# A subtraction on GpSimd in four pieces of 256 columns instead of one of 1024

## The chip and the metric

The kernel runs on one core of a Trainium2 chip. Its time is the device time of one execution in microseconds. In the profile PE is TensorE (PEld its weight loads), DVE is VectorE, ACT is ScalarE, POOL is GpSimd, and SP is SyncE, which only issues DMAs here.

## What is computed

One layer of a hybrid decoder over 512 tokens of width 1024, in float32:

```
h = rms_norm(x, norm_mix)
(hq, hf, hi, hg, nq, kc, vc, ksl, vsl, kwn, vwn, ngate, gate_a, gate_b) = split(h @ w_in)
y_a = hgrn2_mixer(hq, hf, hi, hg, ...) @ w_branch_a
y_b = nsa_mixer(nq, kc, vc, ksl, vsl, kwn, vwn, ngate, ...) @ w_branch_b
mixed = sigmoid(gate_a) * y_a + sigmoid(gate_b) * y_b
x = x + mixed @ w_out
h = rms_norm(x, norm_mlp)
x = x + square(relu(h @ w_up)) @ w_down
```

`hgrn2_mixer` is a gated linear recurrence with 4 heads of 128; `nsa_mixer` is causal attention with 8 query heads, 2 key/value heads of 64 and three branches (compressed blocks, selected blocks, window). `w_in` has 6936 columns, `w_up` is 1024 x 4096, `w_down` 4096 x 1024.

## The kernel before

All weights pass through the core as 127 **chunks** of 128 partitions x 1024 columns of float32 (512 KB), in a fixed order. A matmul in float32 is made of three in the faster type `fp32r`: an operand is split into a high part (rounded to `fp32r`) and a low part (what is left), and `three()` (L362 to L366) multiplies high x high, high x low and low x high into one PSUM bank. A chunk of a plain projection (`project()`, L368) holds eight tiles of 128 x 128 and gives 24 matmuls of 512 columns.

A chunk goes through three engines:
- SyncE loads it into one of four slots of `wraw` (L274), once the chunk four before has been split (`w_split`).
- GpSimd splits it (`split()`, L291): a copy to `whi` in `fp32r` (L292), a wait for that copy (`w_hi`), and a subtraction `wlo = wraw - whi` (L294), whose end raises `w_split`. `whi` and `wlo` have two slots each, so a split begins only when TensorE has used the chunk two before (`w_used`, L300 and L342), and runs while TensorE works on the chunk in between. Chunk 1 has code of its own, in halves of 512 columns (L305 to L311). In the attention stage GpSimd's queue also holds 64 `scale` steps (L327) between some of the splits.
- TensorE waits for `w_split` (`take()`, L352; in the loops of the MLP L773 and L805).

The order of the chunks: `f0 q0 f1 q1 f2 q2 f3 q3`, `i0` to `i3`, `kc vc ks kw nq0` to `nq3`, `m0` to `m2`, `g0 c00 g1 c01 g2 c10 g3 c11`, `ga0` to `ga7`, `gb0` to `gb7`, `ab0` to `ab7`, `wo0` to `wo7`, and 64 of the MLP in two halves of 16 up and 16 down. "Chunk 2" is `f1`. A `c` chunk gives only eight short matmuls (`hidden()`, L575), `m2` only 24 of 280 columns.

VectorE's work around this, as far as it is spoken of below:
- The first sums of squares, L1100 and L1101; a fold of a constant, L1113.
- `start_head()` (L1126 to L1132): the gates of the recurrence for one head. `scaled()` (L1108) reads a finished projection out of PSUM and frees its bank; the next projection but one waits for that (`claim()`, L355).
- `advance()` (L1172): one level of the recurrence, three multiplications in SBUF: L1180 (totals), L1182 (`k_dec`, 1024 elements) and L1183 (`q_dec`, 1024 elements). Behind it stand `keep_near` (L1190), `norm` (L1214) and `leave_stat` (L1221), which frees the bank that a later statistics matmul (L388) of TensorE claims.
- In `ab` and `wo`: L1451 adds the two gated branches, ACT rounds the sum to `hhi` (L1041), `mix_low` (L1439) forms the low part; the first `wo` chunk waits for `mix_lo` before each of its eight tiles.
- In the up stages: L1485 (from PSUM), L1487 (two inputs in SBUF), then ACT's rounding (L1063) and L1490 (two inputs in SBUF).

Of the kernel before, what the change touches and what calls it, by code (L numbers as in the profile page):

```python
# [25 lines left out]
F32 = mybir.dt.float32  # L26
# [3 lines left out]
ALU = mybir.AluOpType  # L30
# [47 lines left out]
def build_block(nc, xT, w, oh, masks, ident_in, small_in, w2, rel, scratch, skewed, out):  # L78
    with ExitStack() as ctx:
        base = (nc.sbuf_base + 31) // 32 * 32  # L80

        def at(name, kb, shape, dt=F32):

            return nc.alloc_sbuf_tensor_at(name, shape, dt, offset=base + int(kb * 1024))

        def sem(name):
            return ctx.enter_context(nc.semaphore(name))
# [16 lines left out]
        wraw = at("wraw", 36.5, [P, NRAW, CW])  # L104
        wsp = at("wsp", 52.5, [P, 2, NSPLIT, CW], F32R)
        whi, wlo = wsp[:, 0], wsp[:, 1]
# [75 lines left out]
        w_split = sem("w_split")  # L182
# [82 lines left out]
        def p_tile(t, g, n):  # L265
            return p_ring[:, t % 4, g, 0:n] if t % 4 < 3 else p_last[g][:, 0:n]
# [4 lines left out]
        @block.sync  # L271
        def _(sp):
            def load(c, slot):
                sp.dma_start(wraw[:, slot, :], w[c]).then_inc(w_landed[slot], 16)  # L274

            load(0, 0)
            for n in range(4):
                sp.dma_start(x0[:, 2 * n:2 * n + 2, :], xT[:, 2 * n:2 * n + 2, :]).then_inc(x_in[n], 16)
            for c in range(1, FIRST):
                if c >= NRAW:  # L280
                    sp.wait_ge(w_split, c - NRAW + 1)
                load(c, c % NRAW)
            with sp.Fori(0, (N_CHUNKS - FIRST) // 4) as i:
                for j in range(4):
                    sp.wait_ge(w_split, 4 * i + (FIRST + j - NRAW + 1))
                    load(4 * i + (FIRST + j), (FIRST + j) % NRAW)


        @block.gpsimd
        def _(pool):  # L290
            def split(c, raw, two):  # L291
                pool.tensor_scalar(whi[:, two, :], wraw[:, raw, :], 1.0, 0.0, ALU.mult, ALU.add).then_inc(w_hi, 1)  # L292
                pool.wait_ge(w_hi, c + 1)
                pool.tensor_tensor(wlo[:, two, :], wraw[:, raw, :], whi[:, two, :].bitcast(F32),  # L294
                                   ALU.subtract).then_inc(w_split, 1)

            def split_straight(c):
                pool.wait_ge(w_landed[c % NRAW], 16 * (c // NRAW + 1))
                if c >= NSPLIT:
                    pool.wait_ge(w_used, c - NSPLIT + 1)  # L300
                split(c, c % NRAW, c % NSPLIT)

            split_straight(0)
            pool.wait_ge(w_landed[1], 16)
            for half in range(2):  # L305
                c = slice(512 * half, 512 * half + 512)
                pool.tensor_scalar(whi[:, 1, c], wraw[:, 1, c], 1.0, 0.0, ALU.mult, ALU.add).then_inc(
                    half_split, 1)
                pool.wait_ge(half_split, 2 * half + 1)
                pool.tensor_tensor(wlo[:, 1, c], wraw[:, 1, c], whi[:, 1, c].bitcast(F32), ALU.subtract).then_inc(  # L310
                    half_split, 1)  # L311
            pool.wait_ge(half_split, 4)
            pool.sem_inc(w_hi, 1)
            pool.sem_inc(w_split, 1)
            for c in range(2, AT["gb2"] + 1):
                split_straight(c)


            def scale(t):
                gi, qb = divmod(t, 4)  # L320
                i, b = divmod(gi, 2)
                n = (qb + 1) * P
                pool.wait_ge(w_ready, t + 1)
                for g in range(2):
                    p_ = p_tile(t, g, n)
                    c = 3 * (4 * g + i) + 1 + b
                    pool.tensor_scalar(p_, p_, rinv[:, t % 4, g:g + 1], gate3[:, qb, c:c + 1], ALU.mult, ALU.mult  # L327
                                       ).then_inc(p_scaled[g], 1)

            for t in range(NT + 2):  # L330
                if t in GB_AFTER:
                    split_straight(AT[GB_AFTER[t]] + 1)
                if t < NT:
                    scale(t)
            for c in range(AT["gb7"] + 2, POOL_FIRST):
                split_straight(c)

            with pool.Fori(0, (N_CHUNKS - POOL_FIRST) // 4) as i:
                for j in range(4):
                    c = POOL_FIRST + j  # L340
                    pool.wait_ge(w_landed[c % NRAW], 16 * i + 16 * (c // NRAW + 1))
                    pool.wait_ge(w_used, 4 * i + (c - NSPLIT + 1))  # L342
                    pool.sem_inc(w_open, 1)
                    split(4 * i + c, c % NRAW, c % NSPLIT)
# [1272 lines left out]
```

## Time and profile before

| | |
|---|---|
| median of 3 runs | 817.58 us (817.57 to 817.68) |
| the profiled execution | 817.72 us, of which the span from first to last instruction is 815.9 us |
| PE busy | 799.5 us, 98% of the span |
| PEld busy | 635.4 us, 78% |
| POOL busy | 490.3 us, 60% |
| DVE busy | 414.9 us, 51% |
| ACT busy | 193.9 us, 24% |
| granted TensorE clock | 1.000 throughout |

A timeline row gives the start and the duration of an instruction in microseconds, the engine, its line, what it writes and reads with shapes, how many were merged into the row, and in brackets how long the engine was idle before it and what released it. A duration of an instruction includes time in which it was issued but held up. Matmuls overlap, so PE's pace is read from the starts of rows that follow each other: 0.23 us for 512 columns.

### The profile page before, as it was taken

To read this page: it belongs to the slowest core of one execution; us is meant where nothing else is said; L and a number is where in the kernel's file an instruction comes from. 1 tells how busy PE (TensorE), PEld (TensorE's weight loads), DVE (VectorE), ACT (ScalarE), POOL (GpSimd) and SP (SyncE) were. 2 spreads that over 40 slices of the span, in tenths; PEclk is the share of its full clock that TensorE was granted. 3 is DMA by queue.
4 is the path that set the end of the run, shared out by engine and by line. 5 is a ranking of instruction groups with operands and counts; after the bars stand their busy time and mean duration, and the time that the engine had idled before them with its cause. 6 is when DMAs were issued, how large, how long until landed. Compare 5 with 4: busy or idle time off the path is not lost.

```text
span 815.9 us, 12340 instructions
## 1 busy us (share of the span) xinstructions
PE 799.5 (98%) x4632; PEld 635.4 (78%) x4632; DVE 414.9 (51%) x565; ACT 193.9 (24%) x397; POOL 490.3 (60%) x324
## 2 busy tenths in 40 slices
PE   8999999998999999999999999999999999999998
PEld 6788877987778566567878888888888888888886
DVE  6696485834465454543887766672000376650000
ACT  5100753312411455545112122220000122210000
POOL 4656644567454565464666666666666666776663
PEclk9999999999999999999999999999999999999999
DMA  7334221233422100004223222223332233233320
GB/s 248 105 126 168 96 79 55 78 116 117 154 78 78 53 27 27 27 27 181 98 84 103 99 83 103 90 90 104 103 100 82 101 104 98 82 103 129 119 86 26
DMA packets 22973, 78.01 MB, mean 96 GB/s; under 512 B 2659, under 2 KB 2923, under 8 KB 22804
## 3 DMA queue, kind: packets, MB, share of 16 engines
q1 hardware_dynamic: 18864, 68.69, 24.8%
q10 hardware_dynamic: 4068, 8.75, 3.0%
q8 instruction: 29, 0.48, 0.2%
q14 instruction: 12, 0.10, 0.0%
HBM read 75.31 MB, written 4.21 MB: 97 GB/s over the span
## 4 chain that ended last, share of the span: by engine, by line
PE 90%; DVE 5%; POOL 2%; DMA 1%; issue 1%; ACT 1%; SPq 0%; DVEq 0%; POOLq 0%; ACTq 0%
PE bank L364 25%; PE bank L366 24%; PE bank L365 24%; PE bank L694 3%; PE bank L706 3%; PE bank L727 2%; PE bank L444 1%; PE bank L446 1%; PE bank L445 1%; DMA wraw<-in_w 1%; PE bank L388 1%; POOL wsp L294 1%; DVE f L1129 1%; PE bank L493 1%; PE bank L716 1%
## 5 line engine op out<-in xcount | busy, mean ns | idle before, releaser
L294 POOL TENSOR_TENSOR wsp<-wraw,wsp 128x1024 fp32r<-128x1024 f32 x126 | 309.6, 2457 | 10.5
L292 POOL TENSOR_SCALAR wsp<-wraw 128x1024 fp32r<-128x1024 f32 x126 | 136.6, 1084 | 255.7 <-PE bank L366 165.3
L364 PE MATMUL bank<-hhi,wsp 128*128 128x512 f32 x352 | 141.2, 401 | 7.3 <-POOL wsp L294 2.5
L365 PE MATMUL bank<-hlo,wsp 128*128 128x512 f32 x352 | 137.4, 390 | 0.0
L366 PE MATMUL bank<-hhi,wsp 128*128 128x512 f32 x352 | 137.3, 390 | 0.0
L364 PE MATMUL bank<-ghi,wsp 128*128 128x512 f32 x256 | 100.3, 392 | 0.0
L366 PE MATMUL bank<-ghi,wsp 128*128 128x512 f32 x256 | 99.7, 390 | 0.0
L364 PE MATMUL bank<-uhi,wsp 128*128 128x512 f32 x256 | 99.7, 389 | 0.0
L365 PE MATMUL bank<-glo,wsp 128*128 128x512 f32 x256 | 99.7, 389 | 0.0
L365 PE MATMUL bank<-ulo,wsp 128*128 128x512 f32 x256 | 99.6, 389 | 0.0
L366 PE MATMUL bank<-uhi,wsp 128*128 128x512 f32 x256 | 99.6, 389 | 0.0
L364 PEld LDWEIGHTS bank<-hhi,wsp 128*128 128x128 f32 x352 | 66.0, 188 | 28.0 <-issue 6.4
L366 PEld LDWEIGHTS bank<-hhi,wsp 128*128 128x128 f32 x352 | 66.1, 188 | 14.3
L365 PEld LDWEIGHTS bank<-hlo,wsp 128*128 128x128 f32 x352 | 66.2, 188 | 12.5
L1487 DVE TENSOR_TENSOR u_ring<-t_ring,r_ring 128x512 f32<-128x512 f32 x32 | 57.2, 1787 | 1.1
L364 PEld LDWEIGHTS bank<-ghi,wsp 128*128 128x128 f32 x256 | 48.0, 188 | 11.9 <-issue 1.5
L364 PEld LDWEIGHTS bank<-uhi,wsp 128*128 128x128 f32 x256 | 48.1, 188 | 10.2 <-issue 0.3
L366 PEld LDWEIGHTS bank<-ghi,wsp 128*128 128x128 f32 x256 | 48.1, 188 | 10.1
L366 PEld LDWEIGHTS bank<-uhi,wsp 128*128 128x128 f32 x256 | 48.1, 188 | 10.1
L365 PEld LDWEIGHTS bank<-ulo,wsp 128*128 128x128 f32 x256 | 48.1, 188 | 9.9
L365 PEld LDWEIGHTS bank<-glo,wsp 128*128 128x128 f32 x256 | 48.1, 188 | 9.7 <-issue 0.2
L1490 DVE TENSOR_TENSOR ulo<-u_ring,uhi 128x512 f32 x32 | 38.6, 1206 | 32.5 <-ACT uhi L1063 32.5
(241 smaller groups left out, 1024.5 us busy)
## 6 DMA issues: line engine op xcount, KB each, us to landing
wraw<-in_w SPq DMA_DIRECT2D x127, 512.0 KB, 3.2
x<-in_xT SPq DMA_DIRECT2D x4, 512.0 KB, 7.5
bias_skewed<-bias_lines ACTq DMA_DIRECT2D x1, 2048.0 KB
bias<-bias_skewed ACTq DMA_DIRECT2D x1, 2048.0 KB, 9.0
x<-in_xT ACTq DMA_DIRECT2D x1, 2048.0 KB, 8.4
out<-x ACTq DMA_DIRECT2D x8, 256.0 KB, 2.0
cst<-in_w ACTq DMA_DIRECT2D x1, 96.0 KB
ohs<-in_oh ACTq DMA_DIRECT2D x1, 82.5 KB
```

Source lines behind the costliest of these rows:

```text
L292: pool.tensor_scalar(whi[:, two, :], wraw[:, raw, :], 1.0, 0.0, ALU.mult, ALU.add).then_inc(w_hi, 1)
L294: pool.tensor_tensor(wlo[:, two, :], wraw[:, raw, :], whi[:, two, :].bitcast(F32), ALU.subtract).then_inc(w_split, 1)
L364: pe.matmul(out_, wh, mh, start=first, stop=False)
L365: pe.matmul(out_, wh, ml, start=False, stop=False)
L366: return pe.matmul(out_, wl, mh, start=False, stop=last)
L388: pe.matmul(to[:, 0:n], matrix, squares, start=True, stop=True).then_inc(stat_out, 1)
L444: pe.matmul(to, hh, wh[:, c], start=k == 0, stop=False)
L694: pe.matmul(score_bank(t, g)[:, 0:n], qn[rows, i, qb * P:qb * P + P], keys[b][rows, 0:n], start=True, stop=True).then_inc(s_done[g], 1)
L706: last = pe.transpose(bank[4 + g][:, kb * P:kb * P + P], p_tile(t, g, S)[:, kb * P:kb * P + P], ident[:])
L727: last = pe.matmul(bank[6][64 * g:64 * g + 64, 256 * half + c:256 * half + 256], v_sw[:, kb, b * P + g * 64:b * P + g * 64 + 64], pt[:, g, ...
L1487: dve.tensor_tensor(u_ring[:, s, :], t_ring[:, s, :], r_ring[:, s, :], ALU.mult).then_inc(u_f, 1)
L1490: dve.tensor_tensor(ulo[:, 4 * i + j, :], u_ring[:, s, :], uhi[:, 4 * i + j, :].bitcast(F32), ALU.subtract).then_inc(u_lo, 1)
```

## The change

The subtraction of `split()` is issued as four instructions of 256 columns each, one behind the other without a wait between them, and the last of them raises `w_split`. The bytes read and written, the semaphores and their counts are the same. `split()` serves 126 of the 127 chunks; chunk 1, which has its own code, is as before. The copy of L292 stays one instruction of 1024 columns. The lines behind it move down by two: the subtraction is L296 in the changed kernel.

```diff
                 pool.wait_ge(w_hi, c + 1)
-                pool.tensor_tensor(wlo[:, two, :], wraw[:, raw, :], whi[:, two, :].bitcast(F32),
-                                   ALU.subtract).then_inc(w_split, 1)
+                for n in range(4):
+                    q = slice(256 * n, 256 * n + 256)
+                    last = pool.tensor_tensor(wlo[:, two, q], wraw[:, raw, q], whi[:, two, q].bitcast(F32), ALU.subtract)
+                last.then_inc(w_split, 1)
```

## Rows read from the trace of the kernel before

**Rows 1.** The page, busy time, share of the span and instructions of each engine.

```profile
PE 799.5 (98%) x4632; PEld 635.4 (78%) x4632; DVE 414.9 (51%) x565; ACT 193.9 (24%) x397; POOL 490.3 (60%) x324
```

**Rows 2.** Pool's groups by form: busy us, mean ns, idle before.

```profile
L294 POOL TENSOR_TENSOR wsp<-wraw,wsp 128x1024 fp32r<-128x1024 f32 x126 | 309.6, 2457 | 10.5
...
L327 POOL TENSOR_SCALAR p_ring<-p_ring,cst 128x128 f32<-128x128 f32 x16 | 7.0, 447 | 4.8 <-DVE cst L1401 4.5
```

**Rows 3.** Timeline of POOL, first subtraction of chunk 1 and the copy behind it.

```profile
14.52 1.28 POOL L310 TENSOR_TENSOR wsp<-wraw,wsp 128x512 fp32r<-128x512 f32 x1
...
15.76 1.61 POOL L307 TENSOR_SCALAR wsp<-wraw 128x512 fp32r<-128x512 f32 x1
```

**Rows 4.** Timeline of DVE in the same stretch.

```profile
15.05 3.38 DVE L1100 TENSOR_TENSOR xsq<-xsq 128x1024 f32<-128x1024 f32 x2 [1.10 <-ACT xsq L854]
...
16.92 3.73 DVE L1100 TENSOR_TENSOR xsq<-xsq 128x1024 f32<-128x1024 f32 x2
```

**Rows 5.** Timelines of PE (chunks started as their split ends) and POOL.

```profile
24.36 0.50 PE L364 MATMUL bank<-hhi,wsp 128*128 128x512 f32 x1 [0.56 <-POOL wsp L294]
...
168.45 0.58 PE L364 MATMUL bank<-hhi,wsp 128*128 128x512 f32 x1
...
177.98 0.50 PE L364 MATMUL bank<-hhi,wsp 128*128 128x512 f32 x1
...
187.45 0.50 PE L364 MATMUL bank<-hhi,wsp 128*128 128x512 f32 x1 [0.37 <-POOL wsp L294]
...
196.88 0.50 PE L364 MATMUL bank<-hhi,wsp 128*128 128x512 f32 x1 [1.54 <-POOL wsp L294]
...
165.68 2.35 POOL L294 TENSOR_TENSOR wsp<-wraw,wsp 128x1024 fp32r<-128x1024 f32 x1
...
175.58 2.35 POOL L294 TENSOR_TENSOR wsp<-wraw,wsp 128x1024 fp32r<-128x1024 f32 x1
```

**Rows 6.** Timelines of POOL, DVE and PE where g0 is split.

```profile
155.70 2.40 POOL L294 TENSOR_TENSOR wsp<-wraw,wsp 128x1024 fp32r<-128x1024 f32 x1
...
155.87 2.25 DVE L1180 TENSOR_TENSOR tot<-tot 128x8 f32<-128x8 f32 x1 [1.16 <-PE bank L530]
...
158.04 1.21 DVE L1182 TENSOR_TENSOR k_dec<-k_dec,tot 128x1024 f32<-128x1024 f32 x1
...
159.17 2.06 DVE L1183 TENSOR_TENSOR q_dec<-q_dec,tot 128x1024 f32<-128x1024 f32 x1
...
158.75 0.40 PE L364 MATMUL bank<-hhi,wsp 128*128 128x512 f32 x1
```

**Rows 7.** Timelines of DVE and PE, two statistics matmuls.

```profile
108.75 2.05 DVE L1180 TENSOR_TENSOR tot<-tot 128x512 f32<-128x512 f32 x1 [0.63 <-PE bank L493]
...
114.86 0.67 PE L388 MATMUL bank<-sq,pair_ones 128*128 128x512 f32 x1 [0.57 <-DVEq L1221]
...
139.28 1.10 PE L388 MATMUL bank<-sq,pair_ones 128*128 128x512 f32 x2
```

**Rows 8.** Timelines of DVE and PE, the wait at 53.96.

```profile
50.48 1.95 DVE L1130 SCALAR_TENSOR_TENSOR k_dec<-e,f 128x512 f32<-128x512 f32 x1
...
53.96 0.47 PE L364 MATMUL bank<-hhi,wsp 128*128 128x512 f32 x1 [0.33 <-DVEq L1111]
```

**Rows 9.** Timelines of DVE and PE, the wait in wo0.

```profile
419.55 2.87 DVE L1451 TENSOR_TENSOR rstd<-gates 128x512 f32<-128x512 f32 x1
...
423.07 0.50 PE L364 MATMUL bank<-hhi,wsp 128*128 128x512 f32 x1 [0.86 <-DVE hlo L1439]
```

**Rows 10.** Timelines of PE and POOL in an up stage.

```profile
485.42 0.39 PE L364 MATMUL bank<-ghi,wsp 128*128 128x512 f32 x1
...
490.86 0.43 PE L364 MATMUL bank<-ghi,wsp 128*128 128x512 f32 x1
...
485.78 1.06 POOL L292 TENSOR_SCALAR wsp<-wraw 128x1024 fp32r<-128x1024 f32 x1 [1.30 <-PE bank L366]
...
492.56 2.81 POOL L294 TENSOR_TENSOR wsp<-wraw,wsp 128x1024 fp32r<-128x1024 f32 x1
```

## The prediction

> **What bounds the kernel now.** I read four views. First the page: TensorE is busy for 98% of the span, so nearly every microsecond is matmul time that this change doesn't touch; it can only widen or narrow the roughly 16 us in which PE stands idle [rows 1]. Second, Pool's group: the subtraction that is cut is one row of 126 instructions of 2.46 us on average, 309.6 us in all [rows 2]. A chunk feeds 24 matmuls, which take 5.44 us (PE starts chunks at 485.42 and 490.86), and one copy and one subtraction fit in that; so most splits have slack, and an average says nothing. Third, the timeline of PE: which chunks does it start the moment their subtraction ends? Fourth, the timelines of DVE and Pool side by side, since the two hold each other up.
>
> **What the rows show of Pool against DVE.** The first `L1100` on DVE (both inputs in SBUF) is issued at 15.05, while Pool's 512-column subtraction runs from 14.52 to 15.80; the next `L1100` starts at 16.92, so the first took 1.9 us [rows 3, 4]. The work alone is about 1.1 us (1024 columns take 1.21 with what surrounds them [rows 6]), thus it ran from 15.80 to 16.92, held until Pool's instruction ended. Pool's next instruction, `L307`, has no wait ahead of it and was issued at 15.76, yet took 1.61 us, against 1.06 for a copy of twice its width elsewhere [rows 10]: it was held by DVE in turn.  So: a DVE instruction with two SBUF inputs and a Pool instruction exclude each other whole, and DVE gets in at the boundary between two Pool instructions even when these stand back to back. DVE instructions that read PSUM are not held. That is the mechanism of this change. It makes four boundaries of one: DVE's waits get shorter, and Pool's split, with up to three DVE instructions let in, gets longer.
>
> The Trainium skill, "SBUF — State Buffer", section "Who interferes with whom", says the same of the lock: one DVE instruction with two SBUF inputs and a GpSimd one that reads SBUF fully block each other for a whole instruction. It adds that issue order decides; that is rival B below.
>
> **Cost of the cut itself.** Undisturbed, 512 columns take 1.28 us and 1024 take 2.35 [rows 3, 5], so 2.09 ns a column and 0.21 us fixed; with 2.40, as elsewhere [rows 6], 0.16 fixed. A 256-column piece is then 0.73 to 0.75 us. Back-to-back Pool instructions overlap by 0.04 (15.76 against 15.80) [rows 3]. Four pieces: 2.80 to 2.88 us, 0.4 to 0.53 over the uncut one. I take +0.5 us a chunk. Ends: 0 if the start of a piece hides wholly under the one before, and +0.95 if each has the 0.32 us that `L327` leaves (447 ns for 128 columns, less 128 at the copy's 1.0 ns) [rows 2]. Of about 63 us more on Pool nearly all lies under matmuls. On the path it stands at these places:
> - Chunk 2 (PE at 24.36, 0.56 idle on `L294`), `g3` (187.45, 0.37 idle) and `ga0` (196.88, 1.54 idle) are waited for; `g2` at 177.98 starts 0.05 after its subtraction ends (175.58 + 2.35 = 177.93) [rows 5]. Each pays 0.5, chunk 2 and `ga0` 0.05 more for small DVE instructions let in (`L1113` and `L1114`; `L1300`): 2.1.
> - `g1` starts at 168.45 and its subtraction ends at 168.03 (165.68 + 2.35): 0.42 of slack, less 0.06 of signal; 0.5 costs 0.15.
>
> The Trainium skill, "GPSIMD Engine Reference", section "2.1 Instruction dispatch", says that each Q7 core starts the next Pool instruction as soon as its own share of the last is done. By that some of the fixed part would be hidden and the sum above would go toward rival C; the 0.04 us of overlap is all that the rows show of it.
>
> **What DVE's intrusion costs.** Chunk `g0` is split at 155.70 and PE starts it at 158.75, 0.65 after the subtraction ends at 158.10 [rows 6]. Today three `advance` instructions wait behind it: `L1180` (8 columns, 2.25 us, nearly all waiting), then `L1182`, 1.21 us and 1.13 from its start to the next one's, and `L1183` of the same size (2.06, since it meets Pool's next copy). With four pieces they get in between: piece 1 to 156.43, `L1180` to 156.53, then three pieces with their start hidden (about 0.55 each) and the two long ones, 156.53 + 1.65 + 2.26 = 160.44, whatever order they win in. PE starts at 160.50 instead of 158.75: +1.75. This is the largest term.
>
> Two statistics matmuls wait for the end of the same chain [rows 7]: at 114.86 (0.57 idle) and at 139.28 (0.32 after the matmul before, where 0.23 is the pace). At 108.75 `L1180` is held to 110.25 today and the chain then runs freely. With pieces it starts at 109.3, but each of the three now waits for one piece: 109.3 + 0.55 + 0.55 + 1.13 + 0.55 + 1.13 = 113.2 against 113.06 today. +0.15 at each, 0.3 together; if DVE's back-to-back instructions won every time it would be -0.4 and -0.1.
>
> **What it gives back.**
> - PE at 53.96 waits 0.33 (0.48 over its pace) for a DVE chain in which `L1130` needs 1.95 us from 50.48, 1.4 of it held [rows 8]. Held by one piece each, its instructions end over 1 us earlier: -0.48, all of that wait.
> - At 423.07, in `wo0`, PE idles 0.86 us because `L1451` (419.55, 2.87 us) sits behind the subtraction [rows 9]. With pieces it ends at about 420.8 instead of 422.4, but the two `mix_low` behind it each wait for a piece: the second is ready near 423.0, its matmul goes at 423.1 instead of 423.9: -0.8.
> - Behind `ga0` PE waits once more for DVE (`L1315`), which is then bound by PE's own matmul: -0.1.
>
> **Sum.** 2.1 + 0.15 + 1.75 + 0.3 = 4.3 lost, 1.4 given back: +2.9 us. The profiled run took 817.72 us (span 815.9 and 1.8 around it), 0.14 over the median of 817.58. 817.72 + 2.9 = 820.6.
>
> **What must stay hidden.** Where two DVE instructions meet a split in every tile (`ab`, `wo` and both up stages: 48 chunks), Pool starts at 485.78 and PE wants the result at 490.86 [rows 10]. One copy and its signal 1.14, four pieces 2.85, twice 0.41 for a DVE instruction let in (the 2.81 us row against 2.40): 4.81 of 5.08. About 0.25 us is left. SyncE's loads and the `scale` steps queue behind the longer split too; loads are issued four chunks ahead, and in the attention stage Pool is idle after each split until DVE has the next sums.
>
> **The rivals.**
> - B, *no gap between pieces* (chance 0.08): Pool's next piece, already issued, beats the waiting DVE instruction, as "issue order decides" would have it. Then DVE waits 0.5 longer everywhere: nine places by 0.5 (chunk 2, 53.96, 114.86, 139.28, `g2`, `g3`, `ga0`, the wait behind `ga0`, 423.07) and 0.5 at `c00` and `g1`, none at `g0`: +5 us, 822.7. Against it speak `L1100`/`L307`.
> - C, *pieces nearly free* (0.15): with +0 a chunk only `g0` still pays, 1.6, and DVE's chains give 1.5 back: 817.9, no change that shows.
> - D, *the loop fills up* (0.09): if a piece set costs over +0.75, the 0.25 us above is used up and 48 chunks pay the excess. At the far end of 0.95: 48 x 0.2 = 9.6, and 7 places 0.45 more each, 3.2: 833. Its first microseconds, at 0.8, give 824.
> - E, the other side: *DVE wins and Pool is not caught* (0.08). If the long `advance` instructions at 156 don't get in ahead of the last pieces, or the split is still over before 158.75, the 1.75 goes; with pieces of no extra cost and DVE winning at 114.86, the gains stand alone: 0.5 + 0.6 + 0.1 + 0.1 + 1.0 = 2.3 less, 815.4. It decides from where `g0` is not waited for and a piece set costs under +0.1.
> - That the change does nothing is excluded: there are four instructions where one was.
>
> **How the numbers follow.** The forecast has 0.60; at its own bounds (+0.45 to +0.6 a chunk) it is 820 to 821.5. The range of 817.0 to 824.0 takes in B, C and the near part of D and leaves out E and the far D. 0.2% is 1.6 us, about what a measurement of this kernel can tell from no change. Faster: 0.07 (most of E). Same: C, a forecast whose `g0` term falls out (+1.15), the rest of E: 0.22. Slower: 0.71.
>
> **What would show it.** In the changed profile, `L296` has 504 instructions of some 0.75 us, longer where DVE gets in; from the first piece's start to the last one's end 2.85 undisturbed. PE's first matmul of `g0` has an idle time of about 1.7 us that names Pool; `g3` and `ga0` show 0.9 and 2.0; the wait at 53.96 is gone and that at 423.07 too; `L1487`, held today in half of the up tiles for most of a subtraction, gets shorter on average. PE waits in the up stages would mean D. A `L1180` still held for 2 us would mean B.

## The result, and the profile after

The changed kernel takes 824.38 us (median of 4 runs, 822.93 to 824.59) against 817.58 for the kernel before (817.51 to 817.68): ratio 1.008, 95% interval 1.0065 to 1.0095. The forecast had the sign and the largest step right, but only 2.9 us of the 6.8, and the time lies just above its range. Two of the later executions took 2809 us at a granted clock of 1.000 (one of the kernel before, one of the run with only `ga0` cut); they are left out of all medians and counts below.

The page of the changed kernel, busy time of each engine, and Pool's two groups:

```profile
PE 801.8 (97%) x4632; PEld 636.5 (77%) x4632; DVE 347.0 (42%) x565; ACT 194.2 (24%) x397; POOL 593.8 (72%) x702
...
L296 POOL TENSOR_TENSOR wsp<-wraw,wsp 128x256 fp32r<-128x256 f32 x504 | 415.6, 855 | 10.5
L292 POOL TENSOR_SCALAR wsp<-wraw 128x1024 fp32r<-128x1024 f32 x126 | 133.9, 1063 | 163.0 <-PE bank L368 111.7
```

The subtraction is now 504 instructions and 415.6 us against 126 and 309.6 [rows 2]. DVE's busy time fell from 414.9 to 347.0 us: what it lost is waiting, which the profile counts as busy. PE gained 2.3 us of busy time with the same 4632 matmuls [rows 1]. A matmul does the same work, so its rows must have become longer somewhere; that is the first trace of what the forecast had left out.

What PE waited for, in the changed kernel (total us, times, longest):

```profile
PE bank L366 <- POOL wsp L296: 6.5, 5, 2.3
PE bank L366 <- DVE hlo L1098: 1.8, 1, 1.8
```

Before, Pool's `L294` had 2.5 us in three waits. The second line is the wait at the start of the program, of 0.7 us in the profile before; it was 1.9 to 2.3 us in three other runs in which no chunk ahead of `g0` is cut, so it isn't the cut's. The wait at 53.96 is not in the list any more, and the `mix_low` wait of 0.86 is not either [rows 8, 9].

The split of `g0`, and PE's first matmul on it; DVE first, then Pool, then PE:

```profile
157.51 0.17 DVE L1182 TENSOR_TENSOR tot<-tot 128x8 f32<-128x8 f32 x1 [0.97 <-PE bank L532]
157.60 1.77 DVE L1184 TENSOR_TENSOR k_dec<-k_dec,tot 128x1024 f32<-128x1024 f32 x1
159.29 1.76 DVE L1185 TENSOR_TENSOR q_dec<-q_dec,tot 128x1024 f32<-128x1024 f32 x1
...
157.54 4.77 POOL L296 TENSOR_TENSOR wsp<-wraw,wsp 128x256 fp32r<-128x256 f32 x4
...
162.36 0.50 PE L366 MATMUL bank<-hhi,wsp 128*128 128x512 f32 x1 [1.81 <-POOL wsp L296]
```

Read beside [rows 6]: the 8-column multiplication took 2.25 us and now takes 0.17. The two long ones, which stood behind the whole subtraction, now stand between its pieces, and the four pieces take 4.77 us where four undisturbed ones take 2.78 (ahead of `g3`, at 189.19; ahead of `ga0`, at 199.39, where two small DVE instructions meet them, 2.82). PE, which didn't wait here before, idles 1.81 us. This is the forecast's 1.75.

The new thing is PE's granted clock. Two stretches of each kernel, cut to PE; columns: stretch, length, PE busy and instructions, granted clock, share and rate of the DMAs. First the changed kernel, behind `f1` and behind `ga0`:

```profile
24.50:28.50 4.00, 3.98 (x11) 0.63 0.47 139
202.80:206.40 3.60, 3.60 (x10) 0.53 0.45 150
```

The same places in the kernel before:

```profile
24.50:28.50 4.00, 4.00 (x20) 1.00 0.46 134
196.90:200.50 3.60, 3.60 (x16) 1.00 0.42 146
```

In the changed kernel 10 matmuls go where 16 went. In single rows:

```profile
202.27 0.50 PE L366 MATMUL bank<-hhi,wsp 128*128 128x512 f32 x1 [2.32 <-POOL wsp L296]
202.60 0.39 PE L367 MATMUL bank<-hlo,wsp 128*128 128x512 f32 x1
202.84 0.45 PE L368 MATMUL bank<-hhi,wsp 128*128 128x512 f32 x1
203.09 0.63 PE L366 MATMUL bank<-hhi,wsp 128*128 128x512 f32 x1
203.51 0.63 PE L367 MATMUL bank<-hlo,wsp 128*128 128x512 f32 x1
203.94 0.63 PE L368 MATMUL bank<-hhi,wsp 128*128 128x512 f32 x1
```

PE stood idle 2.32 us, ran three matmuls at 0.23 to 0.33 us from start to start, and then eight at 0.43: the granted clock is at 0.5 of full speed, which is the lower of its two levels, 1.2 GHz, from 203.04 us for 3.41 us. Eight matmuls at 0.43 instead of 0.23 are 1.6 us. The other such stretch stands behind `f1`, from 25.55 us and as long, after PE's idle 0.99 us there and two waits of 0.86 and 0.75 for chunk 1 shortly before. Behind `g0`, where PE idled 1.81 us, there is none.

**Where the 6.7 us of the span went.** I set the start of each of the 2976 matmuls on 512 (or 280) columns in the one trace against its partner in the other, and noted where the distance between them changes. Each step below is that change in us:

| place | forecast | measured |
|---|---|---|
| `f1` | +0.55 | +0.46 |
| `g0` | +1.75 | +2.07 |
| near levels (114.86 to 141) | +0.3 | +0.47 |
| `g1` | +0.15 | 0 |
| `g2`, `g3` | +1.0 | +0.85 |
| `ga0` | +0.55 | +0.82 |
| 53.96 | -0.48 | -0.54 |
| behind `ga0` | -0.1 | -0.08 |
| `wo0` | -0.8 | -0.75 |
| lower clock behind `f1` | 0 | +1.65 |
| lower clock behind `ga0` | 0 | +1.56 |
| first chunks, before `f1` | 0 | -0.30 |
| small steps behind 400 us | 0 | about +0.5 |

Every place that was named is there, with its sign or at nothing; without the two lines on the clock the sum is 3.5.

The small steps stand in the chunks that two DVE instructions meet, and the weight loads show a wait there. In an up stage, Pool's four pieces and the load of the next chunk's first weights:

```profile
493.49 3.73 POOL L296 TENSOR_TENSOR wsp<-wraw,wsp 128x256 fp32r<-128x256 f32 x4
...
497.27 0.19 PEld L366 LDWEIGHTS bank<-ghi,wsp 128*128 128x128 f32 x1
```

The split ends at 497.22 and the load starts 0.05 us later; in these chunks the distance is 0.05 to 0.13 us, where it was 0.7 to 1.5 us before. The matmul itself follows 0.2 us behind the load. So the margin is used up for the weights and not yet for the matmuls. That these loads are what costs the small steps is not shown by a run.

### The profile page after: what moved, and what is told of

Same layout as the page of the kernel before. It is cut to its first block, busy times and chain, and to the rows that moved or that the text cites. A ratio compares the mean times of both kernels' runs of the same rounds, so it can differ in the third digit from the quotient of the medians.

```text
span 822.6 us, 12718 instructions
## 1 busy us (share of the span) xinstructions
PE 801.8 (97%) x4632; PEld 636.5 (77%) x4632; DVE 347.0 (42%) x565; ACT 194.2 (24%) x397; POOL 593.8 (72%) x702
## 4 chain that ended last, share of the span: by engine, by line
PE 92%; POOL 3%; DVE 2%; DMA 1%; issue 1%; SPq 0%; ACT 0%; DVEq 0%; POOLq 0%
PE bank L366 26%; PE bank L367 25%; PE bank L368 25%; PE bank L696 3%; PE bank L708 3%; PE bank L729 2%; POOL wsp L296 2%; PE bank L390 1%; PE bank L446 1%; PE bank L448 1%; PE bank L447 1%; DMA wraw<-in_w 1%; POOL wsp L292 1%; PE bank L495 1%; PE bank L604 1%
## 5 line engine op out<-in xcount | busy, mean ns | idle before, releaser
L296 POOL TENSOR_TENSOR wsp<-wraw,wsp 128x256 fp32r<-128x256 f32 x504 | 415.6, 855 | 10.5
L292 POOL TENSOR_SCALAR wsp<-wraw 128x1024 fp32r<-128x1024 f32 x126 | 133.9, 1063 | 163.0 <-PE bank L368 111.7
L1063 ACT ACTIVATE r_ring<-bank 128x512 f32<-128x512 f32 x32 | 19.1, 598 | 151.6 <-PE bank L368 151.6
L329 POOL TENSOR_SCALAR p_ring<-p_ring,cst 128x128 f32<-128x128 f32 (+2 forms) x48 | 26.3, 559 | 30.4 <-DVE cst L1403 30.1
```

The lines of the kernel that those rows point to most:

```text
L296: last = pool.tensor_tensor(wlo[:, two, q], wraw[:, raw, q], whi[:, two, q].bitcast(F32), ALU.subtract)
L1063: act.activation(r_ring[:, s, :], bank[b][:], ACT.Relu).then_inc(relu_d, 1)
```

## The experiments

The runs were made later, on two chips and in three series, each beside the kernel before. The runs with DVE behind `g0`, with three chunks and a fill, and with the changed kernel again are the third series, on the second chip. There the kernel before itself shows a granted clock of 1.000 in about half of its runs and 0.998 in the others, and its times fall into two groups accordingly: 817.36 (14 runs) and 818.91 (15 runs) beside the first four experiments, 1.55 us apart. That is what one stretch at the lower clock costs. So I give medians of runs with the same clock, and call "a stretch" what separates 1.000, 0.998 and 0.996. A clock of 0.999 or 0.997 I count as 1.000 or 0.998: in the profiled runs with fill and with halves the lower clock also shows from 818.2 and 816.4 us, behind PE's last matmul, where it costs nothing.

My theory after the result: the loss is (1) the later end of six splits for which PE waits, by 0.5 us each through the pieces' own cost, by 2 us at `g0` through DVE; and (2) stretches at the lower clock, which come where PE stood idle. The rivals are with each run.

**One chunk at a time.** In the first three only one chunk is cut, in the fourth all but the six.

```diff
-                pool.tensor_tensor(wlo[:, two, :], wraw[:, raw, :], whi[:, two, :].bitcast(F32),
-                                   ALU.subtract).then_inc(w_split, 1)
+                pieces = 4 if isinstance(c, int) and c == AT["ga0"] else 1
+                for n in range(pieces):
+                    q = slice(CW // pieces * n, CW // pieces * (n + 1))
+                    last = pool.tensor_tensor(wlo[:, two, q], wraw[:, raw, q], whi[:, two, q].bitcast(F32), ALU.subtract)
+                last.then_inc(w_split, 1)
```

> Only the subtraction of ga0 is cut in four; everything else is the kernel before. Theory (the cost on the path is the wait, and a wait of over 2 us there is followed by some 3 us at the lower clock): PE's idle time ahead of ga0 grows from 1.54 to about 2.3 us, the eight or so matmuls behind it start 0.42 us apart instead of 0.23, and the time is +2.3 us. Rival (the lower clock comes from something else that the cut does elsewhere, such as the busier Pool): idle 2.3, no stretch at the lower clock, +0.8 us.

Measured: without a stretch 818.12 (3 runs), +0.76 over the kernel before; with one 819.50 (6 runs, +0.6); two runs at 820.9 had more. Ratio of all runs 1.0014 (1.0003 to 1.0024). The time agrees with 0.8; the idle time doesn't: in the profiled run (820.88) PE idled 1.97 us ahead of `ga0`, 0.43 more than before. The three runs without a stretch spread over 0.7 us, so the step is 0.4 to 0.8. The lower clock is no fixed consequence: 3 of 11 runs had none. Nor does it wait for PE to go on: in the profiled run it shows from 196.38 us, 0.87 us before PE's first matmul on `ga0` at 197.25, and for 6.8 us, twice as long as elsewhere.

```profile
196.40:197.20 0.80, 0.00 (x0) 0.50 0.00 0
197.20:203.20 6.00, 5.95 (x14) 0.50 0.48 145
```

So "is followed by" is too strong, and "some 3 us" is not its only length.

> Only the subtraction of chunk 2 (f1) is cut in four. Theory: PE's idle time ahead of it grows by 0.45 us and the lower clock shows from about 25.5 to 29 us of the span, as in the changed kernel: +2.1 us in all. Rival: the lower clock there depends on the whole start of the program (there PE began its real work 1.8 us after its warm-up matmuls instead of 0.7) and not on this wait: +0.45 us and no stretch at the lower clock.

Same edit with `c == 2`. With one stretch 819.40 (8 runs), +0.49 over the kernel before with one; 3 runs had two (821.2), none had none. Ratio 1.0026 (1.0017 to 1.0034). In the run that was profiled the stretch stood behind `ga0`, whose split was not cut, and none behind `f1`. So the cut of `f1` costs 0.5 at the same number of stretches, and a stretch may come at either place. It also makes them more frequent: all 11 runs had at least one, against 15 of 29 of the kernel before beside them, and with that the ratio of all runs is worth 2.1 us, which is the theory's sum though not at its place. The rival's wait at the start does not decide: the profiled runs with only `ga0` cut, with the delay and with DVE behind `g0` began with 1.9 to 2.3 us of it, and none had a stretch behind `f1`.

> Only the subtraction of g0 is cut in four. Theory (DVE's two long advance multiplications get in between the pieces): PE idles 1.8 us ahead of g0, where it waited for nothing before, the split ends near 160.5 us of the span, and the time is +1.9 us. Rival (the 0.5 us of the cut alone): the slack of 0.65 us holds it and the time is unchanged.

`c == AT["g0"]`. Without a stretch 819.43 (2 runs), +2.07; with one 820.98 (4 runs), +2.07 again. Ratio 1.0031 (1.002 to 1.0043). PE's first matmul on `g0`:

```profile
160.52 0.50 PE L367 MATMUL bank<-hhi,wsp 128*128 128x512 f32 x1 [1.68 <-POOL wsp L297]
```

PE idled 1.68 us, and the rival (0.5 us within the slack) is out. The profiled run had no stretch behind that idle time.

> All subtractions are cut in four but those of f1, g0, g1, g2, g3 and ga0. Theory (these six carry all of the loss): what is left are the gains at 53.96 and 423.07 (0.5 and 0.8) against 0.4 to 0.5 at the statistics matmuls: -0.9 us, 816.7, clock 1.000 throughout. Rival (the busier Pool, 100 us more of it, or its contention with DVE costs PE elsewhere too): at or above the time of before.

`not (isinstance(c, int) and c in (2, 23, 25, 27, 29, 31))`. Without a stretch 817.16 (7 runs), -0.2; with one 818.53 (5 runs), -0.38. Ratio 0.9994 (0.9986 to 1.0003). Matmul by matmul: -0.6 at 53.96, +0.4 in the near levels, -0.75 in `wo0`, and +0.6 in small steps of 0.08 us between 397 and 694 us. So the six carry the loss but for those small steps. I had expected -0.9 and a clock of 1.000 throughout; both missed, since 5 of 12 runs had a stretch (behind the uncut `ga0` in the profiled one). The steps stand where two DVE instructions meet each split, as in the changed kernel.

**Two pieces instead of four.**

```diff
-                for n in range(4):
-                    q = slice(256 * n, 256 * n + 256)
+                pieces = 2 if True else 1
+                for n in range(pieces):
+                    q = slice(CW // pieces * n, CW // pieces * (n + 1))
```

> Every subtraction in two halves of 512 columns. Theory (a DVE instruction gets in at each boundary, in turn with Pool): an undisturbed pair takes 2.52 us, 0.17 more than one, which costs 0.7 at f1, g2, g3 and ga0 together; at g0 only the 8-column L1180 gets in before the last half, the split ends near 158.3 us of the span and PE hardly waits; the wait at 53.96 goes (-0.5), that at 423.07 stays nearly whole. Sum about 0, within 0.5 us of the kernel before at the same number of stretches at the lower clock. Rival (DVE's back-to-back instructions all get in at one boundary): g0 waits 0.6 us or more.

At a clock of 1.000, 817.72 (2 runs) against 817.56: +0.16 (a third run without a stretch, at 0.999, took 817.14), within the 0.5 foreseen; ratio 1.0004 (0.9995 to 1.0014). At 53.96 -0.5, at `wo0` nothing, as foreseen. At `g0` the rival was nearer, 0.56 of idle time. DVE, then Pool's two halves:

```profile
155.18 1.28 DVE L1183 TENSOR_TENSOR tot<-tot 128x8 f32<-128x8 f32 x1 [1.02 <-PE bank L533]
156.39 1.21 DVE L1185 TENSOR_TENSOR k_dec<-k_dec,tot 128x1024 f32<-128x1024 f32 x1
...
155.15 1.29 POOL L297 TENSOR_TENSOR wsp<-wraw,wsp 128x512 fp32r<-128x512 f32 x1
...
156.40 2.33 POOL L297 TENSOR_TENSOR wsp<-wraw,wsp 128x512 fp32r<-128x512 f32 x1
```

Both DVE instructions got in at the one boundary, although the second half came next on Pool's queue. The row of `L1185` starts at 156.39 and that of the second half at 156.40: the one that started first went first, by 0.01 us. The Trainium skill, "SBUF — State Buffer", section "Who interferes with whom", has it that issue order decides who blocks; the trace agrees. Over this whole trace 173 pairs of a two-input DVE instruction in SBUF and a Pool instruction of the splits overlap by more than 0.15 us, and in all 173 the one whose row starts first also ends first (272 of 273 in the changed kernel, the last one a tie).

**Is it the pieces or DVE that makes `g0` late?** As the run with only `g0` cut, with one wait more on DVE:

```diff
             dve.wait_ge(sc_done, SC_128 + 2)
+            dve.wait_ge(w_split, AT["g0"] + 1)
             advance(7)
```

> As the run with only g0 cut in four, but DVE waits until g0's split is over before the three advance multiplications that got in between its pieces. Theory (those three cost g0 its 1.8 us, not the pieces): PE hardly waits ahead of g0 (the cut split ends near 158.6 us of the span), and the time is that of the kernel before within 0.3 us at the same number of stretches at the lower clock. Rival (the pieces are slow in themselves there): PE still idles over 1 us and the time is +1 us or more.

Without a stretch 817.99 (7 runs) against 817.66: +0.3, at the edge of what was foreseen; ratio 1.0001 (0.9992 to 1.001). The four pieces are undisturbed and PE doesn't wait; Pool, then PE:

```profile
155.38 2.82 POOL L297 TENSOR_TENSOR wsp<-wraw,wsp 128x256 fp32r<-128x256 f32 x4
...
158.43 0.40 PE L367 MATMUL bank<-hhi,wsp 128*128 128x512 f32 x1
```

So the 2 us at `g0` are DVE's two long multiplications.

**Is it the cut or any delay?** Nothing is cut; for `ga0` alone Pool does one piece twice:

```diff
+                if isinstance(c, int) and c == AT["ga0"]:
+                    pool.tensor_tensor(wlo[:, two, 0:256], wraw[:, raw, 0:256], whi[:, two, 0:256].bitcast(F32),
+                                       ALU.subtract).then_inc(half_split, 1)
+                    pool.wait_ge(half_split, 5)
```

> The kernel before, uncut, but Pool subtracts the first 256 columns of ga0 once more, with a wait behind it, ahead of the whole subtraction: a plain delay of about 0.8 us. Theory (what ga0 pays is the later end of its split, cut or not): idle 2.3 us ahead of ga0 as in the changed kernel, +0.8 us against the kernel before at the same number of stretches at the lower clock, and such a stretch at least as often as in the kernel before. Rival (the pieces themselves do it): the idle grows but the lower clock is no more frequent than before.

Without a stretch 818.58 (3 runs), +1.0; with one 819.78 (7 runs), +0.8; two runs with more. Ratio 1.0018 (1.0009 to 1.0027). The profiled run shows a single undisturbed piece, and PE behind it:

```profile
194.47 0.72 POOL L295 TENSOR_TENSOR wsp<-wraw,wsp 128x256 fp32r<-128x256 f32 x1
...
197.69 0.50 PE L368 MATMUL bank<-hhi,wsp 128*128 128x512 f32 x1 [2.37 <-POOL wsp L298]
```

0.72 us is the price of a piece; the forecast had 0.73 to 0.75. And that run had 2.37 us of idle time and the full clock behind it, so the idle time alone doesn't decide. Over runs 9 of 12 here and 8 of 11 with `ga0` cut had a stretch, against 40 of 75 of the kernel before in all these series. That difference alone could be chance; with the runs in which `f1` is cut (11 of 11) and the changed kernel (10 of 10) it is 38 of 44.

**Taking the idle time away.** The changed kernel with PE kept busy while it waits:

```diff
+            for n in range(4):
+                pe.matmul(bank[3][:, 0:P], ones[:], ones[:], start=True, stop=True)
             first_projection(2, x_stat)
...
+            for n in range(9):
+                pe.matmul(bank[7][:, 0:P], ones[:], ones[:], start=True, stop=True)
             project("ga0")
```

> The changed kernel, with 4 and 9 small matmuls on ones put on TensorE's queue ahead of f1 and of ga0, where it waits for Pool; they write banks that are written anew later. Theory (TensorE's clock falls after it stood idle): no stretch at 0.5 of the clock behind f1 and behind ga0, granted clock 1.000, 3.2 us less than the changed kernel with two such stretches (824.4), so about 821.2. Rival (the clock falls by something else, such as Pool's or the whole core's load): the stretches stay and the time is as without the fill.

821.21 us, the median of 5 runs: 820.75 to 821.68 in four of them, at a clock of 1.000 or 0.999, and 822.70 in one, at 0.997. Both places run at full clock in the profiled run:

```profile
24.50:30.50 6.00, 6.00 (x33) 1.00 0.34 107
200.00:210.00 10.00, 9.74 (x53) 1.00 0.33 107
```

> The changed kernel itself, beside the kernel before on this chip. Theory: 3.6 us over the kernel before at the same number of stretches at the lower clock, and one to two such stretches in nearly every run, so mostly 822.7 to 824.4. Rival (its excess on the first chip was a matter of that chip): under 821 in most runs.

The changed kernel, run again, took 823.63 in the median (6 runs, 822.58 to 827.4), not one of them at full clock; ratio 1.0069 (1.0051 to 1.0087). With one stretch it was 822.82 (3 runs), 3.65 over the kernel before with one. So its cost is not the first measurement's alone; and filling the idle time takes 2.4 to 3.2 us off, as far as runs from different series compare (ratio 1.0039, 1.0026 to 1.0052, with the fill). The profiled run had 2.33 us of idle time ahead of `ga0` with a stretch and 0.97 ahead of `f1` with none. What is left, 821 against 817.5, is the 3.5 of the table.

**The gains alone.**

```diff
+                pieces = 4 if isinstance(c, int) and c in (6, 7, 56) else 1
```

(chunks `f3`, `q3` and `wo1`; the loop begins eight chunks later so that `wo1` can be told apart.)

> Only the subtractions of f3, q3 and wo1 are cut in four; those hold up the DVE chains for which TensorE waits at 53.96 and 423.07. Theory: -0.5 and -0.8, so -1.3 us against the kernel before at the same number of stretches at the lower clock. Rival (the gain at one place is taken back by the next wait): -0.5 us or less.

Without a stretch 816.03 (3 runs, and 5 with those at 0.999) against 817.56, -1.5, and with one 817.75 (3 runs) against 818.98, -1.2; ratio 0.9982 (0.9972 to 0.9993). The steps are -0.6 at 53.96 and -0.8 at `wo0`, as in the changed kernel.

> The subtractions of f3, q3 and wo1 in four pieces, all others whole, and 6 small matmuls on ones on TensorE's queue ahead of ga0, where it waits 1.5 us for Pool. Theory (the clock falls behind that idle time in about half of the runs, and the fill prevents it): 816.0 us in nearly all runs, clock 1.000 or 0.999, against 817.4 to 819 for the kernel before. Rival (the lower clock comes whatever stands there): as without the fill, a third or more of the runs at 817.7 and a clock of 0.998.

The same with six small matmuls ahead of `ga0`: 816.52 (8 runs, 816.22 to 816.84) against 818.88; ratio 0.9974 (0.9964 to 0.9984), faster than both kernels. At the full clock alone it is -1.1 against 817.66, and 0.5 short of the 816.0 that I expected. All eight runs had the full clock, where 11 of the 20 beside them of the kernel before did not. Without the fill 3 of 8 had a stretch, but in another series, so what the fill adds rests on the kernel before and on the run above. PE's wait ahead of `ga0` is filled but for 0.16 us:

```profile
194.59 1.56 PE L632 MATMUL bank<-ones 128*128 128x128 f32 x12
196.31 0.50 PE L367 MATMUL bank<-hhi,wsp 128*128 128x512 f32 x1 [0.16 <-POOL wsp L297]
```

## Why the prediction was right or wrong

- **What bounds the kernel**: right. PE's idle time and the few chunks that it waits for hold the whole story but the clock.
- **The exclusion between DVE and Pool, read from `L1100` and `L307`**: right, and the boundary of back-to-back pieces lets DVE in; rival B is out (the 8-column multiplication at `g0` takes 0.17 us, not 2). Its reading of "issue order" was wrong: Pool's next piece is queued but its row starts only 0.04 us before the last one ends, so a DVE instruction that already waits started earlier, and by issue order goes first. The exclusion is wider than two SBUF inputs: before, the 64-column `L1281` reads one tile in SBUF and took 2.44 us beside the subtraction at 179.03, where the same form takes 0.20 alone.
- **The price of the cut**: right. 0.72 us a piece and 2.78 to 2.82 for four, against 0.73 to 0.75 and 2.80 to 2.88. Rivals C and D are out. In the up stages the foreseen 0.25 us is there up to the matmul (0.20 to 0.29), but the weight load ahead of it has only 0.05 to 0.13, a wait that the margin left out; about 0.5 us of small steps stand in such chunks.
- **`g0`, +1.75**: right. The split took 4.77 us against 4.74 foreseen, and the copy ahead of it 1.60 instead of 1.41, which was not foreseen; 2.07 in all, shown by the run with only `g0` cut, and shown to be DVE's by the run in which DVE stands behind.
- **`ga0`, +0.55**: short by 0.3. Its copy began 0.3 us later after `g3` than before, on top of the pieces: 0.45 us after the signal that releases it, not 0.15. With only `ga0` cut, or only delayed, the copy is on time, so its own cut isn't the cause. The late copy goes by Pool's count of instructions: it comes after 196 of them (waits included) in all three profiled runs in which everything is cut and, at `ga3`, in the one with all but six; with halves a copy is late by as much after 68. What stands behind the count no run shows.
- **The DVE chains and what is given back**: right within 0.2 in sum, +0.47 and -1.37 against +0.3 and -1.4.
- **The step that failed is the sum itself**, "4.3 lost, 1.4 given back": it priced a longer wait at its own length and took all matmuls behind it at 0.23 us. The granted clock was 1.000 in the one profile at hand and I put no term on it. It cost 3.2 of the 6.8 us: two stretches of 1.6 us, behind two of the places where the cut lengthened PE's idle time (0.56 to 0.99, and 1.54 to 2.32). The fill run shows in its place what the sum priced: with that idle time filled, 821.2 against the forecast's 820.6. The range had room for the rivals' costs, not for this, and none of the rivals was it.
- The time of the kernel before was so even (817.51 to 817.68) that nothing in it spoke of a stretch; in the later series the same kernel has one in 40 of 75 runs. With the wait ahead of `f1` or `ga0` lengthened it is 38 of 44. That part could not have been sized from the rows at hand.
- Without the clock the sum is 3.5 against 2.9: 1.3 too little at `g0`, `ga0`, the near levels and the small steps, 0.7 too much at `f1`, `g1` to `g3` and the first chunks. That the misses partly cancel is luck.

What stays open: what decides in a single run whether the clock falls. Profiles with 2.0 and 2.3 us idle ahead of `ga0` had a stretch, one with 2.37 had none, some with 1.54 had one, and four with 1.6 to 1.8 ahead of `g0` had none there. Whether the weight loads cause the small steps, and what delays the copy of `ga0`, are open too.

## What to carry to other kernels

Cutting an instruction in pieces to let another engine in has two sides: the other engine's waits get shorter, and the cut work is over later, by the pieces' fixed cost and by everything that gets in between. Look for each consumer of the cut work with less slack than that; cut only where the waiter is on the path and the cut one is not (here three chunks of 126, -1.1 to -1.5 us). Measure the slack up to the weight load and not only up to the matmul. Where the tensor engine will wait longer (by 0.4 to 0.8 us here), reckon with a stretch at the lower clock on top, and try to fill the wait with matmuls that nobody reads.

## What the runs showed of the hardware

- A two-input subtraction on GpSimd took 0.72 us for 256 columns, 1.28 for 512, 2.35 for 1024; four pieces back to back 2.78 to 2.82.
- A DVE instruction with two inputs in SBUF that already waits gets in at the next boundary of Pool instructions, also without a wait there. The one whose row starts first goes first, so DVE can go twice in a row when it starts 0.01 us earlier (the run with halves).
- A DVE instruction with one input in SBUF (`L1281`, 64 columns) was held too: 2.44 us beside a subtraction that starts 0.02 us earlier; `L1283`, of the same form, takes 0.20 alone. From the kernel before, Pool, then DVE:

```profile
179.03 2.41 POOL L294 TENSOR_TENSOR wsp<-wraw,wsp 128x1024 fp32r<-128x1024 f32 x1
...
179.05 2.44 DVE L1281 TENSOR_SCALAR hid<-hid 128x64 f32<-128x64 f32 x1
...
181.79 0.20 DVE L1283 TENSOR_SCALAR hid<-hid 128x64 f32<-128x64 f32 x1
```

- The granted clock of TensorE fell to 0.5 for 3.4 us (6.8 in one run) at idle times of 1 to 2.3 us, in some runs and not in others of the same program, from 0.9 us before PE went on to 1.2 us after; one such stretch cost 1.2 to 1.7 us in a stage of 512-column matmuls. With small matmuls on constants in the idle time 8 of 8 runs of one kernel and 4 of 5 of another had none.
